# Undivided h into the feed-forward, square sums on GpSimd and in the gate loop, and another order on VectorE for the recurrent mixer

## Chip, cores and metric

One core of one Trainium2 chip runs the whole program; the metric is its time on the device in microseconds, median of three runs.

## The reference

256 tokens of width 1024 go through two blocks in float32. Cut to what the change touches:

```python
mix = jnp.concatenate([o_rw, o_nsa, o_s5], axis=-1) @ w_out[i]
h = h + rms_norm(mix, post_mix_norm[i])
f = conv_ffn(rms_norm(h, pre_ffn_norm[i]), w_up[i], conv_w[i], conv_b[i], w_down[i])
h = h + rms_norm(f, post_ffn_norm[i])
e = rms_norm(p[i] @ w_ple[i], ple_norm[i])
h = h + sigmoid(h @ w_ple_gate[i]) * e          # then the second block begins with rmsnorm(h)
...
def conv_ffn(x, w_up, conv_w, conv_b, w_down):
    hu = x @ w_up                                # 1024 -> 5632
    hu = depthwise_conv3(hu, conv_w) + conv_b    # over tokens
    gate, up = jnp.split(hu, 2, axis=-1)
    return (gelu(gate) * up) @ w_down
...
# rwkv7_mixer: per token, S = S*d + (S @ -kk) (kk*a)^T + v k^T; o = S r; then a norm per head, and a gate
```

## The kernel before

Everything lies transposed: 128 channels on the partitions, 256 tokens on the free axis, so that `h` is 8 tiles (k = 0..7) of 128x256, and a "tile" of a projection is 128 output columns. TensorE multiplies in three passes on split operands: ScalarE rounds each weight chunk (128x2048) into `ring_hi`, GpSimd subtracts to get `ring_lo`, and the activations are split likewise into `hn_hi` (ScalarE) and `hn_lo` (VectorE). A split tile is 8 x 3 = 24 matmuls. The program is written engine by engine; each engine runs its own list in order and they meet at semaphores. There is no scheduler: the order is that of the code.

PSUM has 8 banks, handed out in turn (`next_bank`, `opened`); the opening of a bank waits until the job that had it before is freed. Every job (a projection tile, a transposition, a mean square) has one. Weight chunks come through a ring of 6 SBUF slots, and ScalarE makes the high parts from `reach(job)`, which is called ahead of its own readings of PSUM, and does one whenever a slot is free.

Four places matter.

**The recurrent mixer** works in 8 segments of 32 tokens, in two halves s = 0, 1. `blocks(s)` on TensorE makes, for each segment q, a bank H and a bank E; `blocks` on VectorE masks and scales them into `HB` and `EB` (for each q three SCALAR_TENSOR_TENSOR on H, then two TENSOR_TENSOR on E). `state(q)` multiplies `EB` by the state of q - 1 on TensorE, and VectorE adds `HB` in three SCALAR_TENSOR_TENSOR. Hence a chain through both engines: state 1, 2, ..., 6. `receptance(s)` is one VectorE addition. `outputs(s)` on TensorE needs the last state.

**The per-layer embedding** `ple(m)`, m = 0..7, is a small product (two matmuls of 256 columns in plain float32 each) whose results ScalarE copies to `eb`. It serves as filler: 0 and 1 stand in the head norm of the mixer, 2 behind the output projection, 3, 4, 5 ahead of the mean square of norm 2, and 6, 7 behind it.

**Norm 1 and norm 2.** After the output projection, norm 1 (post_mix) has its mean square, its root (ScalarE `root`), a reciprocal (VectorE), and `spread`, which puts the reciprocal root over all partitions into a bank `wd`. `add_normed` adds to `h`. Only then come `squares` of the whole `h` (ScalarE), `mean_square` over them (TensorE, 16 matmuls with one output column), root, reciprocal, `spread(2)`; `scaled_parts` multiplies h by gain and by the spread root, and high and low part follow; then `first_tiles` of the feed-forward begins: for each k the hn_hi passes of four tiles, then the hn_lo passes of each.

**Norm 5** ahead of the second block has the same form: the gate loop (`pg` tiles, tanh, two SCALAR_TENSOR_TENSOR) ends, then `squares`, `mean_square(5)`, root, spread, `modulated`. The others (1, 3, 6 to 9) have a shorter form: ScalarE squares tile by tile, VectorE adds tiles 0 to 5 into one (`add_square`, bank `acc`), and the mean square is 6 matmuls.

In the feed-forward of the first block each of the 44 up tiles goes from its bank through ScalarE (`own`, first tap with bias), VectorE (`convolved`, two taps), ScalarE (`gated`, gelu), VectorE (`product`, `act_low`). L547 is the helper of all matmuls, L2361 that of all ScalarE instructions, L1624 and L1631 those of TENSOR_TENSOR and SCALAR_TENSOR_TENSOR on VectorE, L1564 GpSimd's low parts, L1637 reciprocals.

## Time and profile before

| | |
|---|---|
| median of 3 runs | 1370.98 us (1370.95 to 1371.04) |
| the profiled execution | 1372.01 us, its span 1370.3 us |
| TensorE busy | 1294.2 us, 94% |
| GpSimd / ScalarE / VectorE busy | 843.7 / 616.4 / 549.8 us |
| mean granted TensorE clock | 0.958 |

The busy time of TensorE says how little is left to gain in sum; what a stage can give is read from the stretches in which it stands. The granted clock has two levels, 1.00 (2.4 GHz) and 0.50 (1.2 GHz).

### The profile page before, as it was taken

To read this page: it belongs to the slowest core of one execution; us is meant where nothing else is said; L and a number is where in the kernel's file an instruction comes from. 1 tells how busy PE (TensorE), PEld (TensorE's weight loads), DVE (VectorE), ACT (ScalarE), POOL (GpSimd) and SP (SyncE) were. 2 spreads that over 40 slices of the span, in tenths; PEclk is the share of its full clock that TensorE was granted. 3 is DMA by queue.
4 is the path that set the end of the run, shared out by engine and by line. 5 is a ranking of instruction groups with operands and counts; after the bars stand their busy time and mean duration, and the time that the engine had idled before them with its cause. 6 is when DMAs were issued, how large, how long until landed. Compare 5 with 4: busy or idle time off the path is not lost.

```text
span 1370.3 us, 25855 instructions
## 1 busy us (share of the span) xinstructions
PE 1294.2 (94%) x10789; PEld 1210.2 (88%) x10789; DVE 549.8 (40%) x1246; ACT 616.4 (45%) x939; POOL 843.7 (62%) x426
## 2 busy tenths in 40 slices
PE   6997989879999999899999999999999998999998
PEld 5983547668999999899999999999998888999997
DVE  5658686633455571422433302222222224433302
ACT  5530433125555554544544433554544454544431
POOL 7984400026388887554788776846655665788781
PEclk9997989989899999889999999999999999999998
DMA  8759985603355555424455555453648793455550
GB/s 263 198 181 342 337 307 202 200 1 124 112 179 182 175 183 187 154 93 154 155 185 185 169 172 183 134 159 87 192 126 254 237 291 112 144 182 183 168 167 32
DMA packets 232817, 242.82 MB, mean 177 GB/s; under 512 B 9068, under 2 KB 201726, under 8 KB 232702
## 3 DMA queue, kind: packets, MB, share of 16 engines
q1 hardware_dynamic: 232382, 241.08, 53.8%
q8 instruction: 86, 1.41, 0.4%
q14 instruction: 29, 0.24, 0.1%
q10 hardware_dynamic: 320, 0.10, 0.0%
HBM read 240.11 MB, written 1.05 MB: 176 GB/s over the span
## 4 chain that ended last, share of the span: by engine, by line
PE 73%; ACT 1%; DVE 1%; POOL 1%; DMA 1%; issue 1%; ACTq 0%; DVEq 0%
PE banks L547 72%; PE banks L1276 1%; POOL ring_lo L1564 1%; DMA ring<-in_w_kv_dram 1%; DVE banks L1631 0%; ACT ring_hi L2361 0%; DVE hn L1631 0%; ACT hn_hi L2361 0%; PE banks L557 0%; DVE h L1624 0%; DVE h L1631 0%; ACT arena L2361 0%; ACT hn L2361 0%; ACT rs L2361 0%; ACT L2361 0%
## 5 line engine op out<-in xcount | busy, mean ns | idle before, releaser
L1564 POOL TENSOR_TENSOR ring_lo<-ring,ring_hi 128x2048 fp32r<-128x2048 f32 (+1 forms) x176 | 719.1, 4098 | 456.7 <-ACT ring_hi L2361 456.4
L547 PE MATMUL banks<-hn_hi,ring_lo 128*128 128x256 f32 (+1 forms) x1864 | 529.7, 288 | 0.0
L547 PE MATMUL banks<-hn_hi,ring_hi 128*128 128x256 f32 x1696 | 484.5, 290 | 11.1 <-ACT hn_hi L2361 9.5
L547 PE MATMUL banks<-hn_lo,ring_hi 128*128 128x256 f32 x1696 | 445.0, 283 | 0.0
L2361 ACT ACTIVATE ring_hi<-ring 128x2048 fp32r<-128x2048 f32 (+1 forms) x176 | 299.4, 1703 | 175.0 <-PE banks L547 128.5
L547 PEld LDWEIGHTS banks<-hn_hi,ring_lo 128*128 128x128 f32 (+1 forms) x1864 | 367.4, 197 | 0.1
L547 PEld LDWEIGHTS banks<-hn_hi,ring_hi 128*128 128x128 f32 x1696 | 334.9, 197 | 13.1 <-issue 10.8
L547 PEld LDWEIGHTS banks<-hn_lo,ring_hi 128*128 128x128 f32 x1696 | 310.6, 192 | 0.1
L2361 ACT ACTIVATE arena<-banks 128x256 f32<-128x256 f32 (+6 forms) x231 | 90.4, 410 | 259.0 <-PE banks L547 179.9
L547 PEld LDWEIGHTS banks<-arena 64*128 64x128 f32 (+4 forms) x1282 | 119.1, 182 | 68.2 <-issue 48.0
L547 PE MATMUL banks<-arena 128*64 128x128 f32 (+9 forms) x1282 | 146.5, 308 | 28.1 <-issue 13.2
L1631 DVE SCALAR_TENSOR_TENSOR arena<-banks,par,arena 128x255 f32<-128x255 f32 (+1 forms) x187 | 89.3, 480 | 155.7 <-ACT arena L2361 154.0
L547 PE MATMUL banks<-act_hi,ring_hi 128*128 128x256 f32 x528 | 149.6, 283 | 0.0
L547 PE MATMUL banks<-act_hi,ring_lo 128*128 128x256 f32 x528 | 149.4, 283 | 0.0
L547 PE MATMUL banks<-act_lo,ring_hi 128*128 128x256 f32 x528 | 149.4, 283 | 0.0
L2361 ACT ACTIVATE arena<-banks,par 128x256 f32<-128x256 f32 x88 | 49.7, 565 | 122.6 <-PE banks L547 122.5
L547 PEld LDWEIGHTS banks<-act_lo,ring_hi 128*128 128x128 f32 x528 | 101.4, 192 | 0.0
L547 PEld LDWEIGHTS banks<-act_hi,ring_hi 128*128 128x128 f32 x528 | 101.4, 192 | 0.0
L547 PEld LDWEIGHTS banks<-act_hi,ring_lo 128*128 128x128 f32 x528 | 101.4, 192 | 0.0
L1631 DVE SCALAR_TENSOR_TENSOR h<-banks,mod,h 128x256 f32<-128x256 f32 x32 | 15.5, 484 | 134.0 <-PE banks L547 133.9
L2361 ACT ACTIVATE arena<-arena 128x256 f32<-128x256 f32 (+4 forms) x97 | 46.9, 512 | 41.5 <-DVE arena L1624 13.8
L547 PE MATMUL banks<-ring_lo,hn_hi 128*128 128x256 f32 x208 | 58.8, 283 | 0.0
(258 smaller groups left out, 1574.6 us busy)
## 6 DMA issues: line engine op xcount, KB each, us to landing
ring<-in_ada_w_dram SPq DMA_DIRECT2D x48, 1024.0 KB, 8.1
ring<-in_ffn_w_up_dram SPq DMA_DIRECT2D x44, 1024.0 KB, 5.2
ring<-in_w_up_dram SPq DMA_DIRECT2D x22, 1024.0 KB, 5.1
ring<-in_ffn_w_down_dram SPq DMA_DIRECT2D x16, 1024.0 KB, 5.0
ring<-in_w_kv_dram SPq DMA_DIRECT2D x15, 1024.0 KB, 5.4
ring<-in_w_in_dram SPq DMA_DIRECT2D x9, 1024.0 KB, 8.7
ring<-in_w_kv_dram SPq DMA_DIRECT2D x18, 512.0 KB, 3.9
ring<-in_attn_w_q_dram SPq DMA_DIRECT2D x18, 512.0 KB, 3.8
```

The source lines that it names most:

```text
L547: return nc.tensor.matmul(o, l, r, start=start, stop=stop, **k)
L1276: last = nc.tensor.transpose(b[:, br * P:br * P + P], dsc[s][:, x, k * P:k * P + P], ident[:, :])
L1564: led.emit(g.tensor_tensor(low, raw, high.bitcast(F32), ALU.subtract), sem("lo_ready"))
L1631: led.emit(v.scalar_tensor_tensor(out=o, in0=x, scalar=s, in1=y, op0=op0, op1=op1), signal, value)
L2361: led.emit(nc.scalar.activation(o, x, func, **k), signal, value)
```

## The change

Three edits, one in each of the stages named.

First, `h` goes undivided into the feed-forward. VectorE now splits h times gain inside the adding of norm 1 (`add_normed_split` with `next_gain`), so that the feed-forward's first tiles (now three) can begin with k = 0 before the mean square of norm 2 is known. The squares are summed by GpSimd in 7 additions, one pair of matmuls gives the mean square in the midst of the first tiles, and the spread root is copied to `wide_sb`. Each of the 44 up tiles is multiplied by it on VectorE, in its bank, before ScalarE may read it (semaphore `normed`). Four banks stay held back until the first tiles are through.

Second, norm 5 gets the short form: squares in the gate loop, `add_square(5, ...)` on VectorE, 6 matmuls. With it, the accumulation bank `acc` of `projection` is opened after the first four tiles and no longer before them. `ple` 4 to 7 move ahead of the head norm's spread, and 3 behind the spread of norm 1.

Third, on VectorE alone, the recurrent mixer's `block(q)` and `state(q)` are interleaved.

```diff
-            def first_tiles(rnd, jobs, x, ks=tuple(range(KT)), ms=None):
+            def first_tiles(rnd, jobs, x, ks=tuple(range(KT)), ms=None, norm=None):
...
-                if ms is not None:
-                    gathered(ms)
+                if norm is not None:
+                    b_ms = opened(("ms", norm[0]))
...
+                        if t == 0 and n == KT - 1 and norm is not None:
+                            mean_square_of(norm[0], b_ms, norm[1], (0,))
+                        if t == len(todo) - 1 and n == KT - 1 and ms is not None:
+                            gathered(ms)
...
-            ple(1)
+            for m in (1, 4, 5, 6, 7):
+                ple(m)
...
+            def spread_kept(i):
+
+                kept = [held_back() for _ in range(4)]
...
             projection(0, "out", "out", (hn_lo, hn_hi), (1, sqb), (3, 4, 5, 6, 7, 0, 1, 2))
             ple(2)
-            spread(1)
+            kept = spread_kept(1)
...
-                first_tiles(first, tiles[:4], (hn_lo, hn_hi))
-                for t in tiles[4:]:
+                begin = 4 if f else 3
+                first_tiles(first, tiles[:begin], (hn_lo, hn_hi), norm=None if f else (2, sqb))
+                if f == 0:
+                    for bank in kept:
+                        held.remove(bank)
+                    turn_of[0] = kept[0]
+                    spread(2, False)
+                    ada_columns()
+                for t in tiles[begin:]:
...
-            ada_columns()
-            for m in (3, 4, 5):
-                ple(m)
-            mean_square(2, hn)
-            ple(6)
-            ple(7)
-            spread(2)
+            ple(3)
             ffn(0, 1, (3, sqb))
-            projection(2, "pg", "pleg", (hn_lo, hn_hi))
-
-
-            mean_square(5, hn)
-            spread(5)
+            projection(2, "pg", "pleg", (hn_lo, hn_hi), (5, sqb))
...
-            low_parts(order[:10])
+            first_up = split_no["ug", 0, 1] + 1
+            low_parts(order[:first_up])
+            for k in range(1, KT):
+                pool.wait_ge(sem("squares"), square_base[2] + k + 1)
+                led.emit(g.tensor_tensor(sqb[:, 0, :], sqb[:, 0, :], sqb[:, k, :], ALU.add),
+                         sem("squares_summed") if k == KT - 1 else None)
+                led.settle()
...
-            blocks(0)
+            for q in (0, 1, 2):
+                block(q)
+            state(1)
+            block(3)
             receptance(0)
-            for q in (1, 2, 3):
+            for q in (2, 3):
                 state(q)
...
-            blocks(1)
+            block(4)
+            block(5)
+            state(4)
+            block(6)
+            state(5)
             receptance(1)
-            for q in (4, 5, 6):
-                state(q)
+            state(6)
...
                     if k >= 2:
-                        dve.wait_ge(sem("h_copied"), k - 1)
-                        tt(low[:, k - 2, :], x[(k - 2) % 3], high[:, k - 2, :].bitcast(F32), SUB, sem("x_split"))
+                        dve.wait_ge(sem("h_copied"), KT * (rnd - 1) + k - 1)
+                        if next_gain is None:
+                            tt(low[:, k - 2, :], x[(k - 2) % 3], high[:, k - 2, :].bitcast(F32), SUB, sem("x_split"))
+                        else:
+                            stt(low[:, k - 2, :], x[(k - 2) % 3], col(next_gain, k - 2), high[:, k - 2, :].bitcast(F32),
+                                MUL, SUB, sem("x_split"))
...
                     b = take((nm, f, j))
+                    if f == 0:
+                        tt(b[:, 0:T], b[:, 0:T], wide_sb, MUL, sem("normed"))
+                        if between is not None:
+                            act_low(between)
                     dve.wait_ge(sem("conv_own"), conv_base[f] + (4 * (j // 2) + 2 * x + j % 2 if f == 0 else j) + 1)
...
+                if m >= 4:
+                    add_square(5, m - 3, sqb)
...
+            x = norm_slots(1)
+            for k in range(KT):
+                if k == 0:
+                    ple(3)
+                act_.wait_ge(sem("h_ready"), k + 1)
+                high_part(hn_hi[:, k, :], x[k % 3], scale=col("pre_ffn", k))
+                af(sqb[:, k, :], x[k % 3], ACT.Square, sem("squares"))
+                af(h[:, k, :], x[k % 3], ACT.Identity, sem("h_copied"))
             root(2)
-            ple(6)
-            ple(7)
-            high_parts(2, 1, hn_hi)
+            af(wide_sb, take0(("wd", 2))[:, 0:T], ACT.Identity, *freed(("wd", 2)))
             ffn(0)
```

How the lists of the engines change at three places. VectorE in the second half of the recurrent mixer, before (the first two rows are the E of segment 4, the H rows carry head_ones, the row of 3x128 is `receptance`, and x9 are the states 4, 5 and 6):

```order
230 L1624 TENSOR_TENSOR banks<-banks,head_ones 128x384
231 L1624 TENSOR_TENSOR arena<-banks,ident 128x384
232 L1631 SCALAR_TENSOR_TENSOR arena<-banks,arena,head_ones 128x128 x3
233 L1624 TENSOR_TENSOR banks<-banks,head_ones 128x384
234 L1624 TENSOR_TENSOR arena<-banks,ident 128x384
235 L1631 SCALAR_TENSOR_TENSOR arena<-banks,arena,head_ones 128x128 x3
236 L1624 TENSOR_TENSOR banks<-banks,head_ones 128x384
237 L1624 TENSOR_TENSOR arena<-banks,ident 128x384
238 L1624 TENSOR_TENSOR arena<-banks,arena 128x3x128
239 L1631 SCALAR_TENSOR_TENSOR arena<-banks,arena 128x128 x9
```

VectorE at the same place of the changed kernel:

```order
234 L1646 TENSOR_TENSOR banks<-banks,head_ones 128x384
235 L1646 TENSOR_TENSOR arena<-banks,ident 128x384
236 L1653 SCALAR_TENSOR_TENSOR arena<-banks,arena 128x128 x3
237 L1653 SCALAR_TENSOR_TENSOR arena<-banks,arena,head_ones 128x128 x3
238 L1646 TENSOR_TENSOR banks<-banks,head_ones 128x384
239 L1646 TENSOR_TENSOR arena<-banks,ident 128x384
240 L1653 SCALAR_TENSOR_TENSOR arena<-banks,arena 128x128 x3
241 L1646 TENSOR_TENSOR arena<-banks,arena 128x3x128
242 L1653 SCALAR_TENSOR_TENSOR arena<-banks,arena 128x128 x3
```

State 4 now stands ahead of the last block, state 5 ahead of `receptance`, and only state 6 is left at the end.

TensorE from norm 2's mean square to the start of the feed-forward, before, with what each waits for (pT is `ple`, rs the spread):

```order
1197 L547 MATMUL banks<-ones_mean,hn 128x1 [waits squares]
1198 L547 MATMUL banks<-ones_mean,hn 128x1
1199 L547 MATMUL banks<-ones_mean,hn 128x1 [waits squares]
1200 L547 MATMUL banks<-ones_mean,hn 128x1
1201 L547 MATMUL banks<-pT,ring 128x256 [waits h_ready]
1202 L547 MATMUL banks<-pT,ring 128x256
1203 L547 MATMUL banks<-pT,ring 128x256 [waits h_ready]
1204 L547 MATMUL banks<-pT,ring 128x256
1205 L547 MATMUL banks<-ident,rs 128x128 [waits bank_free2,bank_free1,rs_small,bank_free0,h_ready]
1206 L547 MATMUL banks<-ident,rs 128x128
1207 L547 MATMUL banks<-hn_hi,ring_hi 128x256 [waits lo_ready,bank_free5,bank_free6,bank_free4,x_high,bank_free3]
```

TensorE in the changed kernel, in the low passes of the first three up tiles (late is `ada_columns`, a small product that stood elsewhere):

```order
1242 L549 MATMUL banks<-hn_lo,ring_hi 128x256 [waits x_split] x7
1243 L549 MATMUL banks<-ones_mean,arena 128x1 [waits squares_summed,x_split]
1244 L549 MATMUL banks<-ones_mean,arena 128x1
1245 L549 MATMUL banks<-hn_lo,ring_hi 128x256 x17
1246 L549 MATMUL banks<-ident,rs 128x128 [waits rs_small,x_split]
1247 L549 MATMUL banks<-ident,rs 128x128
1248 L549 MATMUL banks<-late 128x28 [waits x_split,bank_free7]
1249 L549 MATMUL banks<-late 128x28 x3
```

The mean square has moved into the first tiles, and the spread behind them. Two tiles further on stands the first row of the sixth up tile (gate tile 3), whose bank, number 3, was last that of the third (up tile 0) and is freed by VectorE's last tap on that one:

```order
1296 L549 MATMUL banks<-hn_lo,ring_hi 128x256
1297 L549 MATMUL banks<-hn_hi,ring_lo 128x256
1298 L549 MATMUL banks<-hn_hi,ring_hi 128x256 [waits bank_free3]
1299 L549 MATMUL banks<-hn_lo,ring_hi 128x256
1300 L549 MATMUL banks<-hn_hi,ring_lo 128x256
```

In the kernel before the first four up tiles lie in four banks, and no tile of the first eight waits for one of them. ScalarE in the changed kernel, from the root of norm 2 (the first row) over the copy to `wide_sb` to the third tile's `own` (row 209, which frees the way to that last tap):

```order
202 L2393 ACTIVATE rs<-banks,drv 128x2 [waits psum_ready]
203 L2393 ACTIVATE arena<-banks 128x256 [waits psum_ready]
204 L2393 ACTIVATE ring_hi<-ring 128x2048 [waits slot_landed0,psum_ready]
205 L2393 ACTIVATE arena<-banks,par 128x256 [waits normed] x2
206 L2393 ACTIVATE ring_hi<-ring 128x2048 [waits slot_landed1,psum_ready]
207 L2393 ACT_TABLE_LOAD
208 L2393 ACTIVATE banks<-arena 128x256 [waits conv_done]
209 L2393 ACTIVATE arena<-banks,par 128x256 [waits normed]
```

Two high parts of weights and a table load now stand between the known root and the third tile's `own`.

## Rows read from the trace of the kernel before

**Rows 1.** The page's chain that ended last, by engine.

```profile
PE 73%; ACT 1%; DVE 1%; POOL 1%; DMA 1%; issue 1%; ACTq 0%; DVEq 0%
```

**Rows 2.** Stretches: busy us of PE, PEld, DVE, ACT, POOL; clock, DMA share, GB/s.

```profile
290.00:300.00 10.00, 6.74 (x40) 5.95 (x40) 3.71 (x12) 0.00 (x0) 4.13 (x1) 0.50 0.01 2
350.00:360.00 10.00, 8.91 (x43) 8.11 (x42) 6.32 (x17) 4.40 (x11) 0.00 (x0) 0.59 0.32 107
580.00:590.00 10.00, 8.18 (x38) 7.86 (x38) 1.76 (x5) 2.67 (x8) 0.00 (x0) 0.51 0.15 52
```

**Rows 3.** Timeline of VectorE and TensorE, recurrent mixer's second half: start, us, what.

```profile
285.01 0.87 DVE L1631 SCALAR_TENSOR_TENSOR arena<-banks,arena,head_ones 128x128 f32<-128x128 f32 x3 [2.36 <-PE banks L547]
...
286.86 0.86 DVE L1631 SCALAR_TENSOR_TENSOR arena<-banks,arena,head_ones 128x128 f32<-128x128 f32 x3
...
291.29 0.87 DVE L1631 SCALAR_TENSOR_TENSOR arena<-banks,arena 128x128 f32<-128x128 f32 x3
...
292.26 1.62 PE L547 MATMUL banks<-arena 128*128 128x128 f32 x6 [4.33 <-issue]
294.88 3.10 PE L547 MATMUL banks<-arena 128*128 128x128 f32 x18 [1.00 <-issue]
...
299.19 3.34 PE L547 MATMUL banks<-arena 128*128 128x32 f32 x24
```

**Rows 4.** TensorE's timeline at the head norm, and ple 3 to 5.

```profile
309.85 1.53 PE L547 MATMUL banks<-ident,gn_small 128*64 128x128 f32 x24 [0.40 <-DVE gn_small L1637]
...
337.90 2.84 PE L547 MATMUL banks<-pT,ring 128*128 128x256 f32 x12
```

**Rows 5.** Timeline of VectorE and TensorE from norm 1 into the feed-forward.

```profile
337.29 0.88 DVE L1631 SCALAR_TENSOR_TENSOR banks<-arena,par,banks 128x256 f32<-128x256 f32 x2 [0.95 <-PE banks L547]
...
343.22 5.77 PE L547 MATMUL banks<-ones_mean,hn 128*128 128x1 f32 x32 [2.48 <-DVE h L1624]
...
354.56 0.55 PE L547 MATMUL banks<-hn_hi,ring_hi 128*128 128x256 f32 x1 [1.09 <-ACT hn_hi L2361]
...
363.92 4.00 PE L547 MATMUL banks<-hn_lo,ring_hi 128*128 128x256 f32 x32
```

**Rows 6.** Timeline at norm 3, which already adds and splits in one loop.

```profile
550.32 0.88 DVE L1631 SCALAR_TENSOR_TENSOR banks<-arena,par,banks 128x256 f32<-128x256 f32 x2 [1.23 <-PE banks L547]
...
552.72 0.49 DVE L1631 SCALAR_TENSOR_TENSOR banks<-arena,par,banks 128x256 f32<-128x256 f32 x1
...
553.90 0.49 DVE L1631 SCALAR_TENSOR_TENSOR banks<-arena,par,banks 128x256 f32<-128x256 f32 x1
...
552.10 0.55 PE L547 MATMUL banks<-hn_hi,ring_hi 128*128 128x256 f32 x1 [1.81 <-ACT hn_hi L2361]
```

**Rows 7.** Timeline of the first feed-forward: VectorE's taps and product, ScalarE.

```profile
400.31 1.00 DVE L1631 SCALAR_TENSOR_TENSOR arena<-banks,par,arena 128x255 f32<-128x255 f32 x2 [1.88 <-ACT arena L2361]
401.42 0.42 DVE L1624 TENSOR_TENSOR act_hi<-arena,banks 128x256 fp32r<-128x256 f32 x1
...
366.51 1.90 ACT L2361 ACTIVATE ring_hi<-ring 128x2048 fp32r<-128x2048 f32 x1
368.43 1.28 ACT L2361 ACT_TABLE_LOAD   x1
...
402.52 0.57 ACT L2361 ACTIVATE arena<-banks,par 128x256 f32<-128x256 f32 x1 [2.04 <-PE banks L547]
```

**Rows 8.** Timeline of ScalarE and TensorE at norm 5.

```profile
579.83 6.70 PE L547 MATMUL banks<-ones_mean,hn 128*128 128x1 f32 x32 [2.66 <-ACT hn L2361]
...
586.57 0.26 ACT L2361 ACTIVATE rs<-banks,drv 128x2 f32<-128x2 f32 x1 [5.23 <-PE banks L547]
...
589.54 0.55 PE L547 MATMUL banks<-hn_hi,ring_hi 128*128 128x256 f32 x1 [1.18 <-ACT hn_hi L2361]
```

**Rows 9.** GpSimd's groups of 128x256 additions, shapes kept apart.

```profile
L1528 POOL TENSOR_TENSOR arena<-arena 128x256 f32<-128x256 f32 x8 | 7.7, 964 | 17.3 <-DVE arena L1624 15.3 <-PE banks L547 2.0
...
L1539 POOL TENSOR_TENSOR arena<-arena 128x256 f32<-128x256 f32 x8 | 5.8, 729 | 12.8 <-DVE arena L1624 12.8
```

141 lines of the change are left out of this document (74 added, 67 removed).

## Prediction

> **What bounds the kernel now.** I read the chain that ended last first: 73% of the span is TensorE's own work [rows 1], so that a change pays only where TensorE stands or runs slowly. Then the stretches of 10 us, for the granted clock: it is 1.00 through most of the run and falls to 0.50, 0.59 and 0.51 in the three stretches shown [rows 2]. These are the recurrent mixer's second half, norm 2 and norm 5, the places of the change. In each, the timeline shows TensorE waiting: 4.33 us ahead of state 5 [rows 3], 2.48 us for the last h of norm 1 and again until 354.56 [rows 5], 2.66 us at norm 5 [rows 8]. Inside the feed-forward, on the other hand, VectorE and ScalarE wait for TensorE: the idle 1.88 and 2.04 us stand ahead of their instructions [rows 7].
>
> **The recurrent mixer.** In the second half, VectorE starts the first block at 285.01. One block takes 286.86 - 285.01 = 1.85 us, and three of them with `receptance` last until 291.29. Then state 4 (0.87), TensorE's state 5 (at 292.26, 1.62), VectorE's state 5 (0.87), and TensorE's state 6 at 294.88, 9.87 us after the first block's start [rows 3]. In the new order two blocks end at 3.75, state 4 at 4.6, the third block at 6.5; TensorE's state 5 (4.7 to 6.3, even at the 1.62 of the low clock) is hidden behind it. VectorE's state 5 ends at 7.35 and TensorE's state 6 begins at 7.45. That is 2.4 us earlier. In the first half, state 1 goes ahead of the fourth block, but that block's banks come free 0.9 us later, and TensorE's transpositions wait for one of them; by the same prices state 2 comes 0.5 us earlier. What follows state 6 on TensorE, up to the end of the row at 299.19 (3.34 us), runs mostly at the low clock. After shorter waits, a little less of it does: bounds are nothing and the full difference, half of 294.88 to 300, 2.5 us; I take 0.4, since a wait of 1.8 us still stands ahead of each of states 5 and 6. Sum: **-3.3 us**, bounds -2.4 and -5.4.
>
> **The ple tiles.** Three take 2.84 us, 0.95 each [rows 4]. Four more now stand ahead of the head norm's spread, where TensorE waited only 0.40 us for VectorE [rows 4]: 3.8 - 0.4 = **+3.4 us**. Where they stood before, they hid in waits that this change removes anyway, so nothing comes back there but what the next part counts. Bounds: +3.0 (clock held up by the work) to +7 (all at the low clock, twice 0.95 each). VectorE's chain behind the spread (three times three instructions), ScalarE's high parts and the weights move with it and keep their distance to TensorE's need.
>
> **Norm 1 to the feed-forward.** Before: from VectorE's first multiplication at 337.29 to the first tile's matmul at 354.56, then four tiles until 367.8 (the low passes, 32 matmuls, begin at 363.92 [rows 5]; at full clock a matmul comes each 0.12 us, a tile of 24 takes 2.88). Four more tiles: the ninth begins at 367.8 + 11.5 = 379.3, which is 42.0 us after 337.29.
>
> After, with time counted from 337.29. Norm 3 has this loop already: TensorE starts 552.10 - 550.32 = 1.78 us after VectorE, and a k costs 553.90 - 552.72 = 1.18 us [rows 6]. The new low part is a SCALAR_TENSOR_TENSOR in place of a TENSOR_TENSOR, some 0.07 us more (0.40 against 0.33 from start to start), and ScalarE has three instructions per k, about 1.1 us, just under VectorE's 1.25. The last k (two fewer multiplications stand in its round) arrives at 1.8 + 7.9 = 9.7. TensorE needs 6 x 0.12 = 0.72 us per k, so it waits for VectorE. Then its high group 0.7, low passes of three tiles with the mean square in them 3.4, spread 0.6, ScalarE's copy to `wide_sb` 0.4: VectorE may begin at 14.8. GpSimd's seven additions hide behind the loop: a 128x256 addition costs 0.73 to 0.96 us [rows 9], under the 1.25 of a k.
>
> The Trainium skill ("SBUF — State Buffer", Who interferes with whom) says that a VectorE instruction with two SBUF inputs contends with a GpSimd instruction that reads SBUF, one with a single SBUF input not. By this rule the new additions would cost the lower price, since VectorE's partners in the loop lie in PSUM; by it the sum would not move, since both prices hide. The two rows are consistent with it, no row here isolates it.
>
> Now the new wait. The sixth up tile has the bank of the third, which VectorE frees with its last tap. On the way stand, from 14.8: ScalarE's high part 1.9, `own` 0.57, two taps 1.0; multiplication 0.43, `own` 0.57; a high part 1.9, the table load 1.28, gelu 0.38, `own` 0.57; two taps 1.0 [rows 7], and about 0.1 at each of the handovers: it is free at about 24.8. TensorE, after 14.9, has only two tiles (5.8 us) and comes at 20.7. It waits **4 us** there, and by what [rows 2] and [rows 5] show (the mean of 0.59 from 350 to 360 means 8.2 us at the low clock, so until 358.2, some 4 us after the matmul at 354.56) it loses 2.0 more. The sixth, seventh and eighth tile follow: the ninth begins at 24.8 + 8.6 + 2.0 = 35.4. Against 42.0: **-6.6 us**. Bounds: without the wait -12.6; with the clock low through the low passes as well, which puts 14.8 up by 2.4, about -4.
>
> Beyond that, 44 multiplications of 0.43 us are added, 19 us, at nothing: their cover is the arrival of tiles each 2.88 us. A tile now goes multiplication, `own`, taps: 0.43 + 0.57 + 1.0 + 0.2 = 2.2 us, with a product (two of 0.42, less overlap, 0.8) 3.0. For four tiles that is 10.5 us, with a high part of weights (1.9) partly on the way 10.7, against TensorE's 11.5. It fits by 0.8 us in four tiles. If the cover goes, each microsecond over 11.5 costs ten (eleven rounds, the last behind the down projection). What is late next then is the bank eight jobs on.
>
> **Norm 5.** Before: TensorE ends the gate's last tile at 579.83 - 2.66 = 577.2, waits, then the 32-record mean square lasts from 579.83 for 6.70 us, at the low clock, the root comes at 586.57, and the next projection begins at 589.54, 2.97 us behind the root [rows 8]. After: the last tanh (0.4) ends at 577.6; five instructions of VectorE, two of them the new additions, end at about 579.4 (0.33 to 0.43 each), the last square at 579.5. Then the table load [rows 7] and its first use (1.28 + 0.2) run on ScalarE beside 12 matmul records (1.4); both end at about 581.1. Root there, and the 2.97 behind it: 584.0, **-5.5 us**. Bounds -4.5 (a slower gate loop) and -7 (clock held).
>
> The later opening of `acc` delays ScalarE's first squares by three tiles' low passes (3 x 0.96 = 2.9 us) in the projections `out`, `pg` and `po`; it then has three or four tiles of 2.88 us to catch up: nothing.
>
> **Sum:** -3.3 + 3.4 - 6.6 - 5.5 = -12.0 us. Against the profiled execution's 1372.01 (span 1370.3 and 1.7 around it) 1360.0, and since the median of the runs is 1370.98, 1.03 lower, the forecast is **1359.0 us**.
>
> **The rivals.** (a) *No wait for bank 3* (or one under 1 us): TensorE's part at the head norm or the first tiles is later than I have it, or the high parts do not fall in the way. For it: ScalarE's high parts are taken only when the slot is free. Against: rows of both instructions lie exactly there in the new list. 1359.0 - 6.0 = 1353.0. (b) *The clock falls in the paced loop* of the first tiles, where TensorE works 0.72 of each 1.25 us, and the ple tiles run low: +2.4 and +1.5 or so, 1363. For it: low clock in all three stretches [rows 2]; against: the same rows show it back after 4 us of dense work, and at the low clock the loop is dense (6 x 0.21 us is 1.3 per k). [...] (c) *The interleaving gives nothing*, since TensorE's own order is as before and the bank waits eat it: 1362.3. (d) The slower one: *the first feed-forward becomes bound by the handovers* between VectorE and ScalarE. The place is `convolved`: if each round has both high parts (1.9 more, 12.6) on the way and the act_low rows fall outside the gaps (0.4 more), a round takes 13.0, ten rounds cost 15 us, and the time is 1374. It decides from 12.7 us a round (12.0 gained over ten rounds), and is measurably slower from 13.0. For it: only 0.8 us of room per round. Against: in [rows 7] ScalarE has 2.04 us idle ahead of `own`, where a high part fits.
>
> **How the numbers follow.** Forecast 0.5, its own range 1356 to 1362; (a) 0.17; (b) 0.13; (c) 0.08; (d) 0.04 fully and 0.08 in part, a round of 11.8 to 12.5, 1362 to 1369. The range takes in (a) with the lower bound of the mixer's clock, 1351, and (b) and (c) up to 1365. A difference of 0.2%, 2.7 us, is about what can be told from none here: under 1368.2 is faster, which all but (d) are: faster 0.93, same 0.03, slower 0.04.
>
> **What would show it.** TensorE's state 6 near 292 in the mixer; TensorE's spread of the head norm near 310, neither earlier nor later than before; the first up tile near 339; then a wait of about 4 us in TensorE ahead of the sixth up tile, released by VectorE's tap; a period of 11.52 us between the products of even j further on, with TensorE never idle; at norm 5 root and next projection 5 to 6 us closer to the last tanh. A period above 11.52 proves (d) right and me wrong; no wait near 358 proves (a).

## The result and the profile after

The changed kernel takes 1360.57 us (median of 5 runs, 1356.60 to 1365.51), before 1370.98 (5 runs, 1370.69 to 1372.16): ratio 0.9931, 95% interval 0.9909 to 0.9952, 10.4 us less. A second set of 6 runs (e12 below) gave 1356.63 against 1371.62: ratio 0.9901, interval 0.9884 to 0.9918, 15.0 us less. The forecast was 1359.0, with a range of 1351 to 1365. The profiled execution took 1360.57, its span is 1358.1 us, 12.2 less than before's 1370.3; mean granted clock 0.965 against 0.958; TensorE busy 1286.5 us against 1294.2.

The page's chain that ended last, of the changed kernel; to be read beside [rows 1]:

```profile
PE 90%; DVE 5%; ACT 2%; issue 2%; POOL 0%; ACTq 0%; DVEq 0%
```

TensorE's own work makes up 90% of that chain, where it was 73%.

The windows of the same stretches as in [rows 2] (the last one moved up by 10 us with the stage), and the one in which the new wait lies:

```profile
290.00:300.00 10.00, 6.45 (x51) 5.74 (x51) 5.70 (x17) 0.00 (x0) 6.40 (x2) 0.83 0.01 2
350.00:360.00 10.00, 10.00 (x87) 10.00 (x86) 3.21 (x8) 5.11 (x6) 4.00 (x2) 1.00 0.44 142
360.00:370.00 10.00, 6.92 (x47) 6.72 (x47) 6.70 (x12) 4.95 (x7) 7.86 (x3) 0.83 0.29 95
570.00:580.00 10.00, 5.94 (x35) 5.41 (x35) 4.62 (x13) 5.31 (x12) 3.91 (x1) 0.73 0.32 107
```

The clock of the mixer's second half is 0.83 where it was 0.50, and the first tiles of the feed-forward run at 1.00 where norm 2 had 0.59. The 0.83 from 360 to 370 is new.

Cut at eight places that both kernels have, the two traces differ like this (us; each stage runs from the place above to its own):

| up to | before | after | difference |
|---|---|---|---|
| VectorE's first block of the mixer, first half | 262.83 | 264.33 | +1.50 |
| its first block of the second half | 22.18 | 22.94 | +0.76 |
| its state 6 | 11.53 | 9.12 | -2.41 |
| TensorE's head centring (head_center) | 6.62 | 5.65 | -0.97 |
| the head norm's spread | 6.69 | 9.40 | +2.71 |
| VectorE's first multiplication of norm 1 | 27.44 | 27.45 | +0.01 |
| ScalarE's root of norm 3, behind the feed-forward | 211.34 | 203.89 | -7.45 |
| TensorE's projection behind norm 5 | 40.91 | 35.58 | -5.33 |
| the end | 780.76 | 779.74 | -1.02 |

The +1.50 stands ahead of every place of the change. It is not an effect of it: in the thirteen other traces of this study the first block begins anywhere from 259.28 to 264.80, with the same instructions ahead of it.

The mixer's second half in the changed kernel's timeline, beside [rows 3]:

```profile
287.27 0.87 DVE L1653 SCALAR_TENSOR_TENSOR arena<-banks,arena,head_ones 128x128 f32<-128x128 f32 x3 [2.37 <-PE banks L549]
...
289.12 0.86 DVE L1653 SCALAR_TENSOR_TENSOR arena<-banks,arena,head_ones 128x128 f32<-128x128 f32 x3
...
296.39 0.87 DVE L1653 SCALAR_TENSOR_TENSOR arena<-banks,arena 128x128 f32<-128x128 f32 x3 [1.38 <-PE banks L549]
291.98 0.91 PE L549 MATMUL banks<-arena 128*128 128x128 f32 x6 [1.78 <-DVE arena L1646]
294.65 3.08 PE L549 MATMUL banks<-arena 128*128 128x128 f32 x18 [1.76 <-DVE arena L1646]
...
298.55 2.87 PE L549 MATMUL banks<-arena 128*128 128x32 f32 x24
```

State 6 on TensorE begins 294.65 - 287.27 = 7.38 us after the first block (9.87 before; the prediction had 7.45), with waits of 1.78 and 1.76 us ahead of states 5 and 6, as expected. The head norm, beside [rows 4], with five ple tiles in one row:

```profile
306.95 4.56 PE L549 MATMUL banks<-pT,ring 128*128 128x256 f32 x20
311.44 1.53 PE L549 MATMUL banks<-ident,gn_small 128*64 128x128 f32 x24
```

The five take 4.56 us, each beginning 0.86 to 0.94 us behind the one before, and the spread has no wait of its own any more. That the mixer's gain and the tiles' price cancel is seen at VectorE's first multiplication of norm 1: it comes 74.56 us behind the mixer's first block, before 74.46 (the first two terms of the forecast, -3.3 and +3.4, give +0.1). Norm 1 and the start of the feed-forward, beside [rows 5] and [rows 6]:

```profile
338.89 0.88 DVE L1653 SCALAR_TENSOR_TENSOR banks<-arena,par,banks 128x256 f32<-128x256 f32 x2 [0.96 <-PE banks L549]
...
340.75 0.36 PE L549 MATMUL banks<-hn_hi,ring_hi 128*128 128x256 f32 x1 [1.04 <-ACT hn_hi L2393]
...
344.33 0.39 PE L549 MATMUL banks<-hn_hi,ring_hi 128*128 128x256 f32 x1 [0.26 <-ACT hn_hi L2393]
344.69 0.73 POOL L1592 TENSOR_TENSOR arena<-arena 128x256 f32<-128x256 f32 x1 [0.48 <-ACT arena L2393]
...
351.16 0.26 ACT L2393 ACTIVATE rs<-banks,drv 128x2 f32<-128x2 f32 x1 [1.70 <-PE banks L549]
353.74 0.38 ACT L2393 ACTIVATE arena<-banks 128x256 f32<-128x256 f32 x1 [2.32 <-PE banks L549]
354.02 1.91 ACT L2393 ACTIVATE ring_hi<-ring 128x2048 fp32r<-128x2048 f32 x1
...
358.25 1.91 ACT L2393 ACTIVATE ring_hi<-ring 128x2048 fp32r<-128x2048 f32 x1
360.18 1.28 ACT L2393 ACT_TABLE_LOAD   x1
...
363.43 0.58 PE L549 MATMUL banks<-hn_hi,ring_hi 128*128 128x256 f32 x1 [3.08 <-DVE arena L1653]
```

TensorE starts 1.86 us behind VectorE (1.78 forecast) and is paced by it (a k each 1.24 us; waits of 0.26), at full clock. GpSimd's additions take 0.73 us, the lower of the two prices in [rows 9]. Then, between the copy to `wide_sb` (353.74) and the tap that frees bank 3, ScalarE makes two high parts of 1.91 us and loads the gelu table (1.28). TensorE stands 3.08 us ahead of the sixth up tile, and its first matmul behind the wait takes 0.58: the clock is at the low level until 366.2.

One thing no step had foreseen. VectorE and GpSimd in the first round:

```profile
366.92 0.42 DVE L1646 TENSOR_TENSOR banks<-arena,banks 128x256 f32<-128x256 f32 x1
367.67 4.51 DVE L1653 SCALAR_TENSOR_TENSOR gsc<-mod,par 128x8 f32<-128x8 f32 x4 [0.33 <-DVE banks L1646]
372.11 0.42 DVE L1646 TENSOR_TENSOR banks<-banks,arena 128x256 f32<-128x256 f32 x1
...
367.32 4.61 POOL L1579 TENSOR_TENSOR ring_lo<-ring,ring_hi 128x2048 fp32r<-128x2048 f32 x1 [2.14 <-ACT ring_hi L2393]
```

Four instructions on 128x8 elements (`second_gains`) last 4.51 us together, the first of them 4.28 us and the other three 0.15 each; the first ends about when GpSimd's low part does (367.67 + 4.28 = 371.95 and 367.32 + 4.61 = 371.93). Before, the same four took 0.39 us, at a place where GpSimd stood still. VectorE's `product` comes twice in a round of four tiles. Here it is at one round's distance, and further on at two rounds' distance:

```profile
402.04 0.42 DVE L1646 TENSOR_TENSOR act_hi<-arena,banks 128x256 fp32r<-128x256 f32 x1
...
412.24 0.42 DVE L1646 TENSOR_TENSOR act_hi<-arena,banks 128x256 fp32r<-128x256 f32 x1
...
453.56 0.42 DVE L1646 TENSOR_TENSOR act_hi<-arena,banks 128x256 fp32r<-128x256 f32 x1
...
476.60 0.42 DVE L1646 TENSOR_TENSOR act_hi<-arena,banks 128x256 fp32r<-128x256 f32 x1
```

From 402.04 to 412.24 VectorE is still making up for its late start and the 4.5 us, and its longest waits there are for ScalarE and none for TensorE, so the 10.20 us between are the handovers' own time for four tiles; later two rounds take 23.04, 11.52 each, TensorE's own time. Norm 5, beside [rows 8]:

```profile
573.53 1.81 PE L549 MATMUL banks<-ones_mean,arena 128*128 128x1 f32 x12 [2.24 <-DVE arena L1646]
575.38 0.26 ACT L2393 ACTIVATE rs<-banks,drv 128x2 f32<-128x2 f32 x1
...
578.36 0.55 PE L549 MATMUL banks<-hn_hi,ring_hi 128*128 128x256 f32 x1 [1.18 <-ACT hn_hi L2393]
```

### The profile page after: what moved, and what is told of

It is laid out like the page before. It is cut to its first block, busy times and chain, and to the rows that moved or that the text cites. A ratio compares the mean times of both kernels' runs of the same rounds, so it can differ in the third digit from the quotient of the medians.

```text
span 1358.1 us, 25788 instructions
## 1 busy us (share of the span) xinstructions
PE 1286.5 (95%) x10741; PEld 1199.3 (88%) x10741; DVE 571.7 (42%) x1287; ACT 618.4 (46%) x953; POOL 845.2 (62%) x433
## 3 DMA queue, kind: packets, MB, share of 16 engines
q8 instruction: 85, 1.39, 0.4%
## 4 chain that ended last, share of the span: by engine, by line
PE 90%; DVE 5%; ACT 2%; issue 2%; POOL 0%; ACTq 0%; DVEq 0%
PE banks L549 88%; DVE arena L1646 1%; PE banks L1291 1%; DVE arena L1653 1%; PE banks L559 1%; ACT ring_hi L2393 1%; ACT arena L2393 0%; DVE banks L1653 0%; DVE banks L1646 0%; POOL ring_lo L1483 0%; ACTq L1401 0%; PE banks L846 0%; ACT hn_hi L2393 0%; ACT hn L2393 0%; DVE hn L1653 0%
## 5 line engine op out<-in xcount | busy, mean ns | idle before, releaser
L2393 ACT ACTIVATE arena<-banks 128x256 f32<-128x256 f32 (+6 forms) x240 | 94.0, 411 | 257.8 <-PE banks L549 176.4
```

What stands on the lines that cost most here:

```text
L2393: led.emit(nc.scalar.activation(o, x, func, **k), signal, value)
```

## The experiments

Each kernel below was timed in turn with the one before; "ratio" is to the kernel before in the same set, whose medians were 1371.60 us (e1 to e4), 1370.12 (e5 to e8) and 1371.62 (e9 to e12), so that medians of different sets are best compared by their ratios. Even so they say little here. The runs of one changed kernel spread by 1.2 to 12.5 us, and the spread goes with the mean granted clock: the changed kernel's 1365.51 had 0.958 and its 1356.60 had 0.967. So for a mechanism I read the stage in which it lies, from the traces. The cleanest is the one from VectorE's first multiplication of norm 1 to the root of norm 3 (norm 1, norm 2, the feed-forward), "FFN stage" below. The stages are each read from one trace:

| kernel | median, us (runs) | ratio, 95% interval | head centring, from first block | FFN stage | root 3 to projection behind norm 5 |
|---|---|---|---|---|---|
| before | 1370.98 (5) | | 40.33 | 211.34 | 40.91 |
| changed | 1360.57 (5) | 0.9931, 0.9909 to 0.9952 | 37.71 | 203.89 | 35.58 |
| e1_order_alone | 1368.66 (12) | 0.9970, 0.9956 to 0.9984 | 38.99 | 208.55 | 40.48 |
| e2_ple_moved | 1370.61 (12) | 0.9992, 0.9980 to 1.0004 | 40.35 | 207.20 | 40.47 |
| e3_norm5_alone | 1366.49 (9) | 0.9962, 0.9946 to 0.9979 | 40.05 | 208.60 | 35.48 |
| e4_high_first | 1355.95 (4) | 0.9880, 0.9861 to 0.9900 | 38.00 | 200.85 | 35.85 |
| e5_all_but_h | 1361.37 (6) | 0.9933, 0.9915 to 0.9951 | 36.52 | 207.05 | 35.52 |
| e6_gains_by_bank | 1355.84 (4) | 0.9893, 0.9876 to 0.9910 | 37.80 | 200.01 | 35.51 |
| e7_double_mul | 1363.36 (5) | 0.9965, 0.9941 to 0.9990 | 36.50 | 212.29 | 35.55 |
| e8_ple_in_states | 1367.43 (12) | 0.9970, 0.9955 to 0.9985 | 36.11 | 215.55 | 35.57 |
| e9_four_in_states | 1356.72 (6) | 0.9881, 0.9851 to 0.9911 | 36.65 | 200.00 | 35.99 |
| e10_two_in_states | 1354.28 (4) | 0.9875, 0.9862 to 0.9887 | 34.49 | 200.00 | 35.64 |
| e11_table_only | 1356.69 (5) | 0.9889, 0.9872 to 0.9905 | 36.75 | 202.04 | 35.31 |
| e12_changed_again | 1356.63 (6) | 0.9901, 0.9884 to 0.9918 | 36.99 | 204.12 | 35.50 |

### e1_order_alone: the mixer's order on VectorE, nothing else

```diff
-            blocks(0)
+            for q in (0, 1, 2):
+                block(q)
+            state(1)
+            block(3)
...
-            blocks(1)
+            block(4)
+            block(5)
+            state(4)
+            block(6)
+            state(5)
```

> The kernel before with the third edit alone: VectorE's order of blocks and states in the recurrent mixer. Theory, from the trace of the changed kernel: in the second half TensorE's state 6 begins 7.4 us after VectorE's first block (9.87 before), and the granted clock is low for some 3 us there instead of 10; in the first half nothing is gained (0 to 0.8 us lost, since state 1 goes ahead of the fourth block and holds back its banks). Time 2 to 2.5 us under before. Rival (c): the shift is eaten up by the banks and by TensorE's own order, and the time is within 0.5 us of before.

Measured: the ratio's interval gives 2.2 to 6.0 us less, so the interleaving is worth something by itself. In the trace the first half gains 0.84 us (the second half's first block comes 21.34 us after the first one, before 22.18) and VectorE's state 6 another 2.4. But at TensorE's head centring only 1.34 are left, since the clock in this execution stays at the low level from 290 to 310: the row of 24 matmuls of 128x32 that took 2.87 us in the changed kernel took 5.33. At VectorE's first multiplication of norm 1 this trace is even 2.4 us behind before's (76.87 us from the first block against 74.46), so that it cannot show where the median's gain comes from. The pair e2 and e5 says more, since ahead of norm 1 they differ only in this order and in when `acc` is opened: the same point comes after 77.46 and 73.62 us, the clock of each included. The order's gain up to state 6 is steady where the clock holds (3.2 us); what the clock adds or takes differs from execution to execution.

### e2_ple_moved: ple 4 to 7 ahead of the head norm's spread

```diff
-            ple(1)
+            for m in (1, 4, 5, 6, 7):
+                ple(m)
...
-            for m in (3, 4, 5):
-                ple(m)
+            ple(3)
             mean_square(2, hn)
-            ple(6)
-            ple(7)
             spread(2)
```

> The kernel before with only the ple tiles 4 to 7 moved ahead of the head norm's spread, on TensorE and ScalarE. Theory: the spread comes 2.7 us later (3.8 us of tiles less the wait they fill), and of that nothing comes back behind norm 1, where TensorE then stands in waits in their place: 2.7 us slower than before, a trace in which the wait ahead of norm 2's mean square and spread is longer by what the tiles took. Rival: they were not hidden where they stood, and leaving them out there gives back 1 us or more, so that the time is under 1.7 us slower.

Measured: not slower. The median is 1 us under before's, the interval (-2.7 to +0.5 us) leaves out the expected +2.7. The trace shows the spread of the head norm 3.0 us later, as expected, and then this, in TensorE's timeline, with ScalarE's root:

```profile
343.89 5.14 PE L547 MATMUL banks<-ones_mean,hn 128*128 128x1 f32 x24 [0.32 <-ACT hn L2359]
349.06 0.26 ACT L2359 ACTIVATE rs<-banks,drv 128x2 f32<-128x2 f32 x1 [3.00 <-PE banks L547]
349.67 1.19 PE L547 MATMUL banks<-ident,rs 128*128 128x128 f32 x4 [0.64 <-DVE rs L1635]
351.95 0.55 PE L547 MATMUL banks<-hn_hi,ring_hi 128*128 128x256 f32 x1 [1.09 <-ACT hn_hi L2359]
```

From the root to the spread it is now 0.61 us, before 352.40 - 349.03 = 3.37: ple 6 and 7 had stood on the path there, on TensorE, behind the known root. And the mean square is through 9.29 us after VectorE's first multiplication, before 11.70: two more tiles (4, 5) stood in the way of TensorE and ScalarE. Not all of these 2.4 us are the tiles': in e1 and e3, which have them there too, the mean square is through after 10.5 and 10.6 us (it takes 4.60 and 4.66 us there, in before's profile 5.77), and against those the tiles' part is 1.3 us. The step from root to spread is 3.37 or 3.38 us in all three. Before's rows of the same view:

```profile
349.03 0.26 ACT L2361 ACTIVATE rs<-banks,drv 128x2 f32<-128x2 f32 x1 [5.41 <-PE banks L547]
352.40 1.06 PE L547 MATMUL banks<-ident,rs 128*128 128x128 f32 x4
```

Together it is 5.1 us less from VectorE's first multiplication to the first up tile (12.21 against 17.27; against the 16.1 of e1 and e3 3.9 less), so that the first up tile comes 2.1 us earlier although the head norm is 3.0 later. My theory, that these tiles lay hidden where they were, was wrong; the rival holds.

### e3_norm5_alone: the short form of norm 5

```diff
-        SUMMED = (1, 3, 6, 7, 8, 9)
+        SUMMED = (1, 3, 5, 6, 7, 8, 9)
...
-            projection(2, "pg", "pleg", (hn_lo, hn_hi))
-            mean_square(5, hn)
-            spread(5)
+            projection(2, "pg", "pleg", (hn_lo, hn_hi), (5, sqb))
```

(with the squares in ScalarE's gate loop, the additions in VectorE's, and the later opening of `acc`)

> The kernel before with only the short form of norm 5 (squares in the gate loop, five additions on VectorE, 6 matmuls, and the accumulation bank opened after the first four tiles in every projection that has one). Theory: root and next projection come 5.3 to 5.5 us earlier, measured from the root of norm 3, and nothing is lost in the projections out, pg and po by the later opening: 5.5 us under before. Rival: part of the 12 us that the whole change gained comes from elsewhere, and this edit alone gives under 4.

Measured: 35.48 us from the root of norm 3 to the projection, 5.43 less than before; the median 5.1 less than before's 1371.60, the interval 2.9 to 7.4. Every kernel with the short form has 35.3 to 36.0 there. Expected and found.

### e5_all_but_h: the three together, without the undivided h

Its diff is that of e1, e2 and e3.

> The kernel before with the three edits of the last runs together: VectorE's order in the mixer, ple 4 to 7 ahead of the head norm, the short form of norm 5. It is the changed kernel without the undivided h. Theory, from the last runs (medians 2.9, 1.0 and 5.1 us under before, 9 in all; ratios 0.9970, 0.9992 and 0.9962, 0.9924 multiplied): 1361 to 1363, which is the changed kernel's time, so that the undivided h with its wait for bank 3 gives about nothing, and its whole worth lies behind that wait. Rival, by the prediction's account (6.6 us for the undivided h together with the way of the ple tiles, 3.4 given up): 1364 or more.

Measured: ratio 0.9933, the changed kernel's own in its first set; but the second set of that one gave 0.9901, which is 4.4 us less. The medians leave open whether the undivided h gives nothing or several microseconds. The stage is clearer: 207.05 us without it (207.20 in e2), 203.89 and 204.12 with it. By these four traces it is worth 3 us, not the 6.6 that the prediction gave it together with what the ple tiles left behind; the rest of the 7.45 is 1.5 for those tiles (208.6 in e1 and e3, 207.1 in e2 and here) and 2.7 of clock: before's own profile has 211.34 in this stage, where e1 and e3, with the same work in it, have 208.6 and a clock of 0.92 and 0.95 from 350 to 360 in place of 0.59. So my statement that it gives about nothing is not confirmed, and that it would give 6.6 isn't either.

### e4_high_first and e11_table_only: what stands ahead of bank 3

```diff
+            reach(("ug", 0, 0))
             root(2)
+            settle()
+            af(drv[:, 21:22], eps_col, ACT.Gelu_apprx_tanh)
             af(wide_sb, take0(("wd", 2))[:, 0:T], ACT.Identity, *freed(("wd", 2)))
```

(e11 has only the two lines behind `root(2)`.)

> The changed kernel, with ScalarE's first high part of feed-forward weights taken before the root of norm 2 (it waits there for the mean square anyway) and the table of the gelu loaded right behind that root by a one-column activation (it waits there for the spread). Both then lie outside the way from wide_sb to the last tap of the third up tile. Theory: that tap comes 3.2 us earlier (1.9 and 1.28), the wait of 3.08 us ahead of the sixth up tile disappears or shrinks below 0.5, the granted clock does not fall behind it (1.4 us), and the time is 4 to 4.5 us under the changed kernel's. Rival: the high part delays root and spread by as much as it saves, and nothing is gained; or the next high part takes its place and half of the wait stays.

> The changed kernel, with only the gelu table loaded behind the root of norm 2, and the high part where the changed kernel has it. Theory: 1.28 of the 3.08 us of waiting for bank 3 are gone, 1.8 are left, and the clock falls a little less long: 1.5 us under the changed kernel; the rest of what e4_high_first gained is the high part's. Rival: the table alone does it, since the high part overlaps with VectorE's work.

ScalarE and TensorE in the timeline of e4_high_first:

```profile
344.78 1.95 ACT L2393 ACTIVATE ring_hi<-ring 128x2048 fp32r<-128x2048 f32 x1
346.63 0.26 ACT L2393 ACTIVATE rs<-banks,drv 128x2 f32<-128x2 f32 x1
347.11 1.28 ACT L2393 ACT_TABLE_LOAD   x1 [0.22 <-ACT rs L2393]
...
356.28 0.39 PE L549 MATMUL banks<-hn_hi,ring_hi 128*128 128x256 f32 x1 [0.47 <-DVE arena L1653]
```

The high part ends where the root's turn comes, the table is there before the spread. The wait for bank 3 is 0.47 us in place of 3.08, and 1.65 with the table alone; in both TensorE then waits 0.6 us for a late `act_low`, which the next section takes up. The FFN stage shortens by 2.0 us with the table and by 3.2 with both, against the mean of 204.0 in the two traces of the changed kernel. The clock stays at 1.00 from 340 to 380 in e4 and e11 alike, so that the 1.4 us of low clock are saved in both; of e11 I had expected only a part of them. So the terms of the prediction's list of what stands ahead of that tap were real, each with its own price. By the ratios e4 (0.9880) stands 7.0 us under the first set of the changed kernel (0.9931) and 2.9 under the second (0.9901); e11 and e12, on one chip, are equal (1356.69 and 1356.63), where 1.5 us less was expected. The medians do not show this gain; the waits do.

### e6_gains_by_bank: the four gains with one input in PSUM

```diff
+                aside = bank_of(("ug", 0, 1))[:, 0:32]
...
+                    copy(aside[:, 8 * n:8 * n + 8], mod[:, c0:c0 + 8])
+                settle()
...
-                    stt(gsc[:, 8 * n:8 * n + 8], mod[:, c0:c0 + 8], 1.0, gn, ADD, MUL, sem("gains"))
+                    stt(gsc[:, 8 * n:8 * n + 8], aside[:, 8 * n:8 * n + 8], 1.0, gn, ADD, MUL, sem("gains"))
```

> The kernel of e4_high_first, with the four gains (128x8) of VectorE calculated from a copy in a PSUM bank: four copies of 128x8 from SBUF into the dead half of a bank, then the same four SCALAR_TENSOR_TENSOR with one input in PSUM and one in SBUF, where both lay in SBUF. Theory: with two SBUF inputs such an instruction stands until GpSimd's low part (4.6 us) is through; with one in PSUM it doesn't. The eight together take under 1.2 us in place of 4.5, act_low comes 3.5 us earlier, the wait of 0.59 us that TensorE had for it is gone, 0.6 us less time than e4_high_first. Rival: the 4.5 us have another reason (a semaphore between the four, or the reading of the small columns itself), and the gains take 4 us again.

VectorE in its timeline; GpSimd's low part runs from 365.14 to 369.77:

```profile
365.49 0.37 DVE L1656 COPY banks<-mod 128x8 f32<-128x8 f32 x4 [0.33 <-DVE banks L1646]
365.89 0.38 DVE L1653 SCALAR_TENSOR_TENSOR gsc<-banks,par 128x8 f32<-128x8 f32 x4
...
365.14 4.63 POOL L1579 TENSOR_TENSOR ring_lo<-ring,ring_hi 128x2048 fp32r<-128x2048 f32 x1 [1.04 <-ACT ring_hi L2398]
```

Eight instructions, 0.78 us from the first start to the last end, in the midst of the low part, where four took 4.51. In e4 TensorE had waited 0.59 us for the late `act_low`; that wait is gone, and the stage takes 200.01 against 200.85. The median doesn't tell it (1355.84 and 1355.95). What made them slow is that both inputs lay in SBUF while GpSimd read SBUF: the copies read the same small columns, and the four keep their semaphore. The Trainium skill ("SBUF — State Buffer", Who interferes with whom) says that a VectorE instruction with two SBUF inputs contends with a GpSimd instruction that reads SBUF. This trace agrees for 128x8: 4.28 us in the changed kernel, 0.17 with one input in PSUM.

### e7_double_mul: the room of a round

```diff
-                        tt(b[:, 0:T], b[:, 0:T], wide_sb, MUL, sem("normed"))
+                        tt(b[:, 0:T], b[:, 0:T], wide_sb, MUL)
+                        settle()
+                        tt(b[:, 0:T], b[:, 0:T], wide_sb, MUL, sem("normed"))
```

> The changed kernel with each of the 44 multiplications by the spread root made twice on VectorE (the second waits for the first; the output is not the reference's, since these tiles are normed twice). It measures the room of a round of four tiles. Account of the prediction: a round takes 10.5 to 10.7 us in VectorE and ScalarE against TensorE's 11.52; with four more multiplications of 0.43 and their handover it takes 12.4, and eleven rounds cost 9 to 10 us over the changed kernel. Rival: the engines overlap more than that account has it (VectorE is busy 7.2 of 10 us there), the period stays at 11.5, and the time is within 1.5 us of the changed kernel's.

VectorE's product in its timeline, two rounds apart:

```profile
437.58 0.42 DVE L1646 TENSOR_TENSOR act_hi<-arena,banks 128x256 fp32r<-128x256 f32 x1
...
461.55 0.42 DVE L1646 TENSOR_TENSOR act_hi<-arena,banks 128x256 fp32r<-128x256 f32 x1
```

23.97 for two rounds, 11.98 each: over TensorE's 11.52, by half of what was expected. The banks between the engines hold the lag back for long; TensorE has no wait from 380 to 450, then 2.6 and 1.4 us and a lower clock (0.98 and 0.93). The stage takes 8.3 us more than in the changed kernel, the ratio 0.9965 against 0.9931 and 0.9901. That this is near the expected 9 to 10 is in part luck: some 5.8 are the two late waits and the low clock behind them, but another 2 are the wait for bank 3 (3.60 us in place of 3.08) and the low clock behind that, 0.83 over 20 us from 360 on, in the changed kernel over 10. Hence a round without the addition costs 11.98 less four times 0.53 to 0.61 (the second multiplication's step in this trace), 9.5 to 9.9 us, near the 10.20 read from the changed kernel's catching up. The room is 1.3 us or more (11.52 less 10.20), not 0.8.

### e8_ple_in_states, e10_two_in_states, e9_four_in_states: the tiles in the states' gaps

e2 had shown what a ple tile costs at the head norm, and [rows 3] where TensorE stands. e8 (on top of e6):

```diff
             state(4)
+            ple(4)
             state(5)
+            ple(5)
             state(6)
...
-            for m in (1, 4, 5, 6, 7):
+            for m in (1, 6, 7):
                 ple(m)
```

> The kernel of e6_gains_by_bank, with ple 4 and 5 taken from the head norm and put on TensorE between the states 4 and 5 and the states 5 and 6 of the recurrent mixer, where TensorE waits 1.78 us each time for VectorE; ScalarE copies them ahead of the high parts that it makes there. Theory: each tile (0.95 us) is hidden in its wait, the head norm's spread comes 1.9 us earlier relative to state 6, and TensorE's clock is no lower: 1.5 to 2 us less time than e6_gains_by_bank. Rival: the tiles, at the low clock and with a wait for their weights or banks, hold up the states, and the time is the same or longer.

TensorE and GpSimd in the timeline of e8:

```profile
290.50 1.03 PE L549 MATMUL banks<-pT,ring 128*128 128x256 f32 x4
292.45 0.91 PE L549 MATMUL banks<-arena 128*128 128x128 f32 x6 [0.92 <-DVE arena L1649]
...
347.07 9.04 POOL L1582 TENSOR_TENSOR ring_lo<-ring,ring_hi 128x2048 fp32r<-128x2048 f32 x2 [18.86 <-ACT ring_hi L2401]
...
351.84 0.55 PE L549 MATMUL banks<-hn_hi,ring_hi 128*128 128x256 f32 x1 [16.39 <-POOL ring_lo L1582]
```

The first part went better than expected: the tile fits into the gap (0.92 us of waiting are left), the clock is 1.00 from 290 to 320 (0.66, 0.83, 1.00 in e6), and the head norm's spread comes 4.9 us earlier. But at the end of norm 1 TensorE then stands 16.39 us for the low part of an up chunk. The second chunk of up weights is issued at 335.48 in e8, at 323.23 in e6. My reading: the weights stream in the order of first use through 6 slots, the ple chunk now comes ahead of the four `out` chunks and the first up chunk, and the second up chunk needs its slot, which is held until ple 3, the last tile (334.42 to 335.45). Two kernels test it. In e10 only the last ple tiles are earlier:

```diff
-            for m in (1, 6, 7):
+            for m in (1, 6, 7, 2, 3):
...
-            ple(2)
             kept = spread_kept(1)
...
-            ple(3)
             ffn(0, 1, (3, sqb))
```

e9 puts four tiles into the gaps (3, 4 and 5, 6), four into the head norm.

> The kernel of e8_ple_in_states, with ple 2 and 3 moved from norm 1 into the head norm, so that 0, 1, 6, 7, 2, 3 stand there and 4 and 5 between the states. It changes the one thing that the theory of the ring names, the time of the last ple tile. Theory: the wait of 16.4 us is gone; against e9 the head norm is 1.9 us later, and the time is 2 us over e9's, 2 to 3 under e6_gains_by_bank. Rival: the wait in e8 comes from ScalarE's or GpSimd's own order, and is there again.

> The kernel of e8_ple_in_states, but no ple tile behind the head norm any more: 3 and 4 stand between the states 4 and 5, 5 and 6 between the states 5 and 6, 0, 1, 2 and 7 in the head norm. In e8 the head norm came 4.9 us earlier than without the two tiles, and then TensorE stood 16.4 us for a low part of feed-forward weights. Theory: the ple weights now stand ahead of the out weights in the ring of 6 slots, so that the second chunk of up weights has their slot, and it was held until ple 3, the last, was through at 334; with the last tile at 307 the chunk is loaded long before it is needed, the 16.4 us are gone, and what e8 had gained stays: 4 to 6 us under e6_gains_by_bank, 1350 to 1352. Rival: two tiles in one gap (1.9 us against 1.78 of waiting) hold the states up by 0.2 us each, and without a tile behind norm 1 TensorE waits there as long as it worked: only 2 us under e6.

Measured: the wait of 16 us is gone in both. The timeline of the engine that issues the transfers, from 300 to 345, of e8 and then of e10:

```profile
335.48 8.37 SPq L1439 DMA_DIRECT2D ring<-in_w_up_dram  x5
```

```profile
305.22 25.05 SPq L1437 DMA_DIRECT2D ring<-in_w_up_dram  x5
```

In e10 the last ple tile ends at 305.19 and the second up chunk is issued at 305.22, as in e8 at 335.45 and 335.48; only the places of ple 2 and 3 differ between the two kernels. The ring is shown. e10 takes 1354.28 us (runs 1353.91 to 1355.12), 2.4 under the changed kernel on the same chip (1356.63), and 17.3 under the one before. Its root of norm 3 lies 271.49 us behind the mixer's first block, in e6 274.69, in the changed kernel 278.45. Its median is the lowest of all, but by the intervals of the ratio (0.9862 to 0.9887 against 0.9884 to 0.9918) it is not set apart from the changed kernel, nor from e4 (0.9861 to 0.9900). e9 is not better, against what I expected: its six runs lie far apart, 1348.27 and 1348.74 at a mean clock of 0.976 and 0.973, 1353.98 at 0.969, and three from 1359.45 to 1360.77 at 0.959 to 0.963. In the traces of e9 and e10 the clock falls from 330 to 340 (0.72 and 0.66, in e6 1.00), at norm 1, where TensorE now stands without its two tiles. And part is given back later: behind norm 5's projection e10 takes 783.78 us and e9 785.69, e6 780.41. In e10 most of it is this wait:

```profile
1014.10 1.92 PE L549 MATMUL banks<-ring,arena 128*32 128x512 f32 x16 [2.53 <-issue]
```

It waits ahead of a matmul that reads a weight slot, in a stretch in which the DMA engines are busy 0.70 of the time and more; e9 has 2.62 us there, e6 no such wait. That the stream of weights is what it waits for there fits, but was not tested.

### e12_changed_again

> The changed kernel once more, on the chip of the three others. Its five runs lay between 1356.6 and 1365.5, those of before between 1370.7 and 1372.2. Theory: the scatter comes from how long the granted clock stays low in the mixer and behind it, and the runs spread by 5 to 9 us again, around 1360 to 1361, with the traces apart already at the first block of the mixer, where no edit stands. Rival: the scatter was one chip's, and the runs lie within 2 us.

Measured: 1355.52 to 1362.62, 7.1 us apart, before on this chip 4.5 (1369.17 to 1373.67, 11 runs). The scatter is there again, and the first block of the mixer begins at 259.28 here, 5 us earlier than in the first profile. Why the two sets of the changed kernel differ by 0.3% (0.9931 and 0.9901, with intervals that overlap) stays open. TensorE's timeline in the mixer's first half, first of the changed kernel's profile, then of this one; the program is the same:

```profile
270.64 2.10 PE L559 MATMUL banks<-ident,arena 128*128 128x128 f32 x9 [1.84 <-DVE arena L1653]
272.53 4.86 PE L549 MATMUL banks<-arena 128*128 128x128 f32 x48
```

```profile
265.58 1.20 PE L559 MATMUL banks<-ident,arena 128*128 128x128 f32 x9 [1.84 <-DVE arena L1653]
266.62 4.11 PE L549 MATMUL banks<-arena 128*128 128x128 f32 x48
```

The same 9 transpositions behind the same wait of 1.84 us take 2.10 and 1.20 us. Five of the eleven traces with the new order have the low level here or, as e4, in the next row but one (the second half's first block then comes 22.9 us after the first, else 21.3), none of the three with the old order, where two waits of 1.07 and 1.39 stand in place of the one of 1.84.

## Why the prediction was right, point by point

**The mixer, -3.3.** State 6 came 7.38 us after the first block (7.45). Where the clock held, it gave about what was taken: at the head centring the traces of e5, e11 and e12 are 3.8, 3.6 and 3.3 us shorter than before's. The first half's 0.5 is 0.84 where the clock holds, and turns into a loss of 0.76 where it falls behind the longer wait, as in the changed kernel's own profile (-2.6 in all). Rival (c) is refuted by e1's interval (2.2 to 6.0 us less) and by the pair e2 and e5.

**The ple tiles, +3.4.** Between 2.7 and 3.0: a tile follows the last one after 0.86 to 0.94 us; the 0.95 read from three held the tail of the last one three times over. The sentence on where they stood was off: they did not hide there. 2.8 us of them stood between root and spread, and 1.3 to 2.4 ahead of the mean square (e2). It did the sum no harm, since the next term counted the whole path from 337.29 on and so took their removal in.

**Norm 1 to the feed-forward, -6.6.** The trace has -7.45 up to the root of norm 3. Step by step: start 1.86 (1.78), period 1.24 (1.25), `wide_sb` known at 353.74 + 0.38 - 338.89 = 15.2 (14.8), bank 3 free at 24.5 (24.8), a wait of 3.08 (4), and 1.4 us of low clock behind it (2.0). Right in each, and still it is a statement about one execution of before, which had 2.7 us more low clock here than e1 and e3. Between kernels without that the undivided h is worth 3.0 and the way of the tiles 1.5, 4.5 together: the steps were right, but that the term came near -6.6 is in part the luck of which execution of before was profiled. Rival (a) is refuted by the wait; without it (e4, e6) the stage is 3 to 4 us shorter, not the 6.0 of that rival. Rival (b) is refuted: with waits of 0.26 to 0.54 us once in each period of 1.24 the clock stayed at 1.00. The Trainium skill ("TensorE: Matmul & The Clock Gate", A second HAM failure mode: psum-queue depth-cycling) tells of a kernel in which short idle times between groups of matmuls made the clock fall again and again. This trace does not show that for gaps of this size. The rival was not absurd, though: in the same trace the like loop of norm 3, behind a wait of 1.81 us, runs at the low level (0.50 from 544 to 550), and behind the 3.08 us ahead of bank 3 it fell as well.

**44 multiplications at nothing.** Right: 11.52 us per round. The handovers take 10.2 (10.5 to 10.7). TensorE has no wait between the one for bank 3 and norm 3. Rival (d) was further away than the 0.8 us of room had it: four more multiplications a round, in e7, cost about half a microsecond a round.

**Norm 5, -5.5.** -5.3 in the changed kernel; 35.3 to 36.0 us in every trace with the short form, 40.5 to 40.9 in those without.

**`acc` later: nothing.** No new wait ahead of norms 1, 3 or 6 to 9.

**Not in the prediction:** the 4.5 us of `second_gains`, which moved from a place where GpSimd stood still to one where it is busy 80% of the time. They were hidden in the changed kernel by the lag that TensorE's own wait had given; with that wait gone (e4) they cost 0.6.

The sum was -12.0 from a profiled execution; the profiled one after has 12.2 less span, with 1.5 lost and 1.0 gained at places that the change doesn't touch. The median lost 10.4 in the first set and 15.0 in the second. With what the comparisons between kernels give for the third term (-4.5 in place of -6.6) the sum would have been about -10: near the first set, 5 short of the second. The forecast of 1359.0 lies between the two medians.
